# Two layers of two hybrid blocks on one core: gated attention's queries and keys turned once per token tile, the bias table stored first, the modulation without a register loop

## The chip, the cores and the metric

The kernel runs on one core of a Trainium2 chip. The metric is the device time of one execution in microseconds; lower is better. The five engines are named as in the profile: PE (TensorE, the matmuls), DVE (VectorE), ACT (ScalarE), POOL (GpSimd) and SP, which here only issues DMAs.

## What is computed

A sequence of 512 tokens of width 2048 goes through two blocks of two layers each, all in float32. The first block's layer is a projection, three kinds of attention (dense, latent, and a neighbourhood attention with a table of relative position biases `rpb`), and an output projection:

```
proj = jnp.einsum('bsd,de->bse', h, w_in)
...
s = jnp.einsum('bqhd,bqnhd->bhqn', qblk, kg).astype(jnp.float32) * scale
s = s + bblk[None].astype(jnp.float32)
...
return x + _rms_norm(y, g_post)
```

The second block's layer is modulated by a vector `c`, and one of its three branches is gated linear attention, with decays summed within chunks of 64 tokens:

```
mod = jax.nn.silu(c) @ w_mod + b_mod
...
b = jnp.cumsum(lac, axis=2)
diff = b[:, :, :, None, :] - b[:, :, None, :, :]
decay = jnp.exp(jnp.where(causal[:, :, None], diff, -jnp.inf))
scores = jnp.einsum('bhtd,bhsd,bhtsd->bhts', qc, kc, decay)
```

`w_mod` is 2048 x 6144 for each of the two layers of the second block, and does not depend on the activations.

## The kernel before

Every engine has its own instruction stream, written out by hand, and the streams meet through counting semaphores (`count(name, ...)`, `wait_ge`, `then_inc`). The main work is the projections. A panel of 512 output columns runs over 16 slices `k` of 128 input rows. For each slice, PE does 12 matmuls of 128x512: four token tiles, and three products each (`L823` to `L825`, and `L818` to `L820` where the result is wanted turned), because every float32 operand is split in a high and a low part. SP loads the weights in pairs of slices into `stage` (ring of 4), ACT takes the high part (`L1307`), DVE the low part (`L1791`), both into rings of 3.

Between the slices stands side work: after the matmuls of slice `k` of panel `p`, PE calls `side1(l, s)` (first block) or `side(l, s)` (second block). A step `s` is one slice; in the first block `s = 16 p + k`, in the second 48 less. ACT and DVE call functions of the same names at the same steps. Tables at the head of the file say which step carries what: `UNIT_AT` and `JOB_AT` the attention of the first block, `SUM_AT` the sums of the modulation, `LEVEL` the levels of gated attention.

Gated attention (second block, `LEVELS = 6` and a diagonal one, so 7 levels, for two pairs `pr` of token tiles, so 28 groups `g` per layer). For each pair and level, PE sums the logarithms of the decays with a 0/1 matrix (`decay_sums`, `L1140`), ACT exponentiates them into `eg` (`take_decays`, `L1680`), DVE multiplies queries and keys `qk_g` by them into `qke` (`decayed`, `L2561`). Then, tile by tile, PE turns the four 128x128 pieces of `qke` with the identity (`level_turns`, `L1208`), ACT copies them from PSUM to `qkT` (`L1724`), PE multiplies them to scores (`level_scores`, `L1221`), DVE masks the scores (`level_mask`, `L2576`), and POOL adds them up (`L2845`). The level steps are 74 to 78, 81 to 94 and 97 to 110. `level_turns(g)` stands in the step of index `g`, `level_scores(g - 1)` in the same one.

POOL also carries the modulation while the first block runs. `mod_panel(l, p, ring)` multiplies 16 slices of 128x512 of `w_mod` (`mod_load`, `L2751`) with the gate vector (`L2764`) and adds them up (`L2769` for the first of a panel, `L2771` for the others). There are 12 panels for each layer. PE sums a finished panel over the partitions (`mod_row_sum`, `L1009`), at the steps of `SUM_AT` for panels 0 to 8; it waits for POOL's last addition, and POOL waits to begin panel `p` until panel `p - 2` is summed, as `macc` has two buffers. POOL starts each layer of this when `CKV_READY` is reached.

The bias table of the neighbourhood attention is padded in `rpb_pad`, a strip at the end of the big buffer `zone`, then stored to `rpb_dram` (`L2791`), and read back in an expanded form by `bias_tiles` (`L2781`, eight DMAs on POOL's queue). ACT's `scores_high` (`L1545`) writes over the same end of `zone` and so waits for the store:

```
if first == 4:
    act.wait_ge(job_ev.sem, job_ev.at(0, l, J_VB + 4))
    act.wait_ge(prep.sem, prep.at(0, l, QPE_READY + 1))
    act.wait_ge(boot_rpb, 32)
```

DVE's low parts (`L2180`) come behind `scores_high`, and PE's first attention scores (`L966`, unit `U_B`, step 51) behind those.

Of the kernel before, what the change touches and what calls it, by code (L numbers as in the profile page):

```python
# [15 lines left out]
P = 128  # L16
# [101 lines left out]
QCT_AT, STATE_AT = 62, 65  # L118
PAST_AT = {67 + 2 * t: t for t in range(TT)}
# [12 lines left out]
SCALED_AT = {(64 if k == 0 else LEVEL[2 * slot_of(k) - 2]): k for k in range(2 * LEVELS)}  # L132
# [84 lines left out]
def build(nc, io, only_first=False):  # L217


    with ExitStack() as ctx:  # L220
# [182 lines left out]
        gt_done = count("gt_done", 0, 28)  # L403
        gte_done = count("gte_done", 0, 28)
# [195 lines left out]
        qcT, qkT = view(ZQ, TT, 2, P), view(ZQ, 2, 4, P)  # L600
# [9 lines left out]
        LEVELB, TURNB, OUTP = bank[4:6], bank[6], bank[7]  # L610
# [186 lines left out]
        def _(pe):  # L797
# [328 lines left out]
            def decay_sums(l, n, level, pr):  # L1126
# [12 lines left out]
                for i in range(2):  # L1139
                    mm = pe.matmul(decay_bank(n)[:, i * 256:(i + 1) * 256], gsum[:, level, :], la[:, 2 * pr + i, :],  # L1140
                                   start=True, stop=True)
# [37 lines left out]
            def past(l, t):  # L1179

                pe.wait_ge(job_ev.sem, job_ev.at(1, l, J_STATE + 2 * t + 1))
                if t == 0:
                    pe.wait_ge(ajob_ev.sem, ajob_ev.at(1, l, 7))
                else:
                    pe.wait_ge(past_ev.sem, past_ev.at(1, l, t))
# [10 lines left out]
            def level_turns(l, g, level, t):  # L1196

                s = g // 2
                if g == 0:
                    pe.wait_ge(past_ev.sem, past_ev.at(1, l, TT))  # L1200
                else:
                    pe.wait_ge(gte_done.sem, gte_done.at(1, l, g))
                if level < LEVELS:
                    pe.wait_ge(ge_done.sem, ge_done.at(1, l, 2 + (s // (LEVELS + 1)) * LEVELS + level + 1))
                for w in range(2):
                    for hp in range(2):
                        src = qk_g[:, t, w, tok(hp)] if level == LEVELS else qke[s % 2][:, t % 2, w, tok(hp)]
                        mm = pe.transpose(TURNB[:, tok(2 * w + hp)], src, ident[:, :])  # L1208
                mm.then_inc(gt_done.sem, 1)

            def level_scores(l, g):

                pe.wait_ge(gte_done.sem, gte_done.at(1, l, g + 1))
# [23 lines left out]
            def side(l, s):  # L1237
# [35 lines left out]
                if 0 <= g < 4 * (LEVELS + 1):  # L1273
                    level_turns(l, g, g // 2 % (LEVELS + 1), 2 * (g // (2 * LEVELS + 2)) + g % 2)
# [25 lines left out]
        def _(act):  # L1300
# [390 lines left out]
            def side(l, s):  # L1691
# [27 lines left out]
                g = LEVEL.index(s) if s in LEVEL else -1  # L1719
                if 0 <= g < 4 * (LEVELS + 1):  # L1720
                    act.wait_ge(gt_done.sem, gt_done.at(1, l, g + 1))
                    if g >= 2:
                        act.wait_ge(gs_done.sem, gs_done.at(1, l, g - 1))
                    act.activation(qkT[:, g % 2, :, :].rearrange("p w n -> p (w n)"), TURNB[:, :], ACT.Copy)\  # L1724
# [58 lines left out]
        def _(dve):  # L1783
# [770 lines left out]
            def decayed(l, k):  # L2554
# [3 lines left out]
                if s >= 2:  # L2558
                    dve.wait_ge(gt_done.sem, gt_done.at(1, l, 2 * (s - 1)))
# [174 lines left out]
        def _(pool):  # L2734
# [9 lines left out]
                           io["c_rpb"].rearrange("l h r c -> (l h r) c")).then_inc(boot_rpb, 16)  # L2744
            pool.wait_ge(boot_dve, 2)
# [38 lines left out]
            for l in range(2):  # L2784
# [85 lines left out]
```

## Time and profile before

| | |
|---|---|
| time, median of 3 runs | 3527.45 us (3526.79 to 3528.84) |
| the profiled execution | 3530.76 us |
| its span on the core | 3528.6 us |
| PE busy | 3432.4 us, 97% |
| DVE, ACT, POOL busy | 54%, 37%, 33% |
| mean granted clock of PE | 0.990 |

The span runs from the first to the last instruction; the 2.2 us between it and the execution's own time lie around it. PE's busy time counts overlapping matmuls once, so it says that PE always has something under way, not that it works at its peak. In the rows below a timeline row has the start, the time taken, the engine, the line and the operation, and in brackets the idle time of the engine before it and what ended it. A float32 matmul shows as two records, a transpose or a matmul of the rounded parts as one.

### The profile page before, as it was taken

How to read it: one execution, taken by the hardware profiler on the slowest of the kernel's cores; microseconds unless marked ns; L12 is line 12 of the kernel's file. 1: busy time of each engine (PE TensorE's matmuls, PEld its weight loads, DVE VectorE, ACT ScalarE, POOL GpSimd, SP SyncE). 2: the span in 40 equal slices, each digit the busy share in tenths (PEclk: the TensorE clock that was granted, in tenths of full speed). 3: DMA queues.
4: the chain of work that ended last, by engine and by line, in shares of the span. 5: the costliest groups of instructions: out<-in, count | busy, mean ns of one | idle time of the engine just before them, and what ended most of it. 6: DMA issues, size and time to landing. Idle time of an engine off the chain costs nothing.

```text
span 3528.6 us, 48194 instructions
## 1 busy us (share of the span) xinstructions
PE 3432.4 (97%) x17244; PEld 2815.9 (80%) x17244; DVE 1903.1 (54%) x3226; ACT 1317.9 (37%) x2173; POOL 1176.6 (33%) x1310
## 2 busy tenths in 40 slices
PE   8959999999999999899999999999999999999998
PEld 7638888888886788788888878878888878878887
DVE  5523486553675346665447445545547535645545
ACT  6113323332551333233337335322336435332233
POOL 0477667674205777777641000012000000002000
PEclk9979999999999999999999999999999999999999
DMA  6444454445673555444567532322446622322345
GB/s 210 144 120 120 156 154 137 133 152 177 215 231 112 144 156 148 137 136 137 197 196 220 158 66 61 98 72 60 138 157 211 189 72 61 99 71 62 120 149 185
DMA packets 225282, 490.40 MB, mean 139 GB/s; under 512 B 24254, under 2 KB 33337, under 8 KB 221224
## 3 DMA queue, kind: packets, MB, share of 16 engines
q1 hardware_dynamic: 188264, 369.13, 33.8%
q0 software_dynamic: 33632, 109.11, 10.9%
q10 hardware_dynamic: 3168, 9.24, 0.7%
q8 instruction: 138, 2.26, 0.3%
q14 instruction: 80, 0.66, 0.1%
HBM read 470.54 MB, written 20.52 MB: 139 GB/s over the span
## 4 chain that ended last, share of the span: by engine, by line
PE 89%; DVE 4%; issue 2%; POOL 2%; DMA 1%; ACT 1%; DVEq 0%; POOLq 0%; another core or an unknown queue 0%; ACTq 0%; SPq 0%
PE bank L823 23%; PE bank L825 22%; PE bank L824 22%; PE bank L986 3%; PE bank L966 3%; PE bank L975 2%; PE bank L818 1%; PE bank L820 1%; PE bank L819 1%; PE bank L949 1%; PE bank L1089 1%; DVE wlo L1791 1%; PE bank L1221 1%; PE bank L1068 1%; PE bank L846 1%
## 5 line engine op out<-in xcount | busy, mean ns | idle before, releaser
L823 PE MATMUL bank<-wlo,act_hi 128*128 128x512 f32 (+1 forms) x3712 | 1480.8, 399 | 9.5 <-DVE wlo L1791 5.7
L825 PE MATMUL bank<-whi,act_lo 128*128 128x512 f32 (+1 forms) x3712 | 1440.3, 388 | 0.0
L824 PE MATMUL bank<-whi,act_hi 128*128 128x512 f32 (+1 forms) x3712 | 1438.7, 388 | 0.0
L1791 DVE TENSOR_TENSOR wlo<-stage,whi 128x1024 fp32r<-128x1024 f32 (+1 forms) x624 | 838.0, 1345 | 776.3 <-ACT whi L1307 765.0
L1307 ACT ACTIVATE whi<-stage 128x1024 fp32r<-128x1024 f32 (+1 forms) x624 | 649.2, 1041 | 961.2 <-PE bank L825 813.8
L823 PEld LDWEIGHTS bank<-wlo,act_hi 128*128 128x128 f32 x3712 | 698.2, 188 | 171.6 <-issue 23.4
L825 PEld LDWEIGHTS bank<-whi,act_lo 128*128 128x128 f32 x3712 | 697.8, 188 | 147.6
L824 PEld LDWEIGHTS bank<-whi,act_hi 128*128 128x128 f32 x3712 | 699.3, 188 | 130.6
L2771 POOL TENSOR_TENSOR macc<-macc,mprod 128x512 f32<-128x512 f32 x360 | 504.0, 1400 | 67.5 <-POOL mprod L2764 67.5
L2751 POOL DMA_DIRECT2D wmod<-in_w_mod x384 | 222.2, 579 | 523.5 <-DVE zone L2128 298.8
L2764 POOL TENSOR_SCALAR mprod<-wmod,csil 128x512 f32<-128x512 f32 x384 | 310.3, 808 | 164.9 <-DMA wmod<-in_w_mod 82.6
L2845 POOL TENSOR_TENSOR zone<-zone 128x512 f32<-128x512 f32 x48 | 61.9, 1290 | 390.6 <-DVE zone L2576 390.6
L1531 ACT ACTIVATE zone<-bank 128x512 f32<-128x512 f32 x128 | 76.6, 598 | 233.4 <-PE bank L975 233.4
L2802 POOL CAST act_hi<-zone 128x256 fp32r<-128x256 f32 x64 | 32.8, 536 | 373.1 <-ACT zone L1462 372.4
L2827 POOL DMA_DIRECT2D macc<-in_gla_w_gate_up x4 | 2.1, 526 | 432.1 <-DVE Y L2411 432.1
L818 PE MATMUL bank<-act_hi,wlo 128*128 128x512 f32 x256 | 111.1, 434 | 0.0
L2095 DVE RECIPROCAL ri<-sm 128x1 f32<-128x1 f32 x128 | 20.5, 160 | 161.9 <-PE bank L986 160.9
L986 PEld LDWEIGHTS bank<-zone 128*128 128x128 f32 x768 | 100.3, 191 | 8.8 <-issue 1.4
L1523 ACT ACTIVATE zone<-bank,nmx,rsq 128x512 f32<-128x512 f32 x64 | 49.8, 779 | 149.1 <-DVE nmx L2087 149.1
L986 PE MATMUL bank<-zone 128*128 128x128 f32 x768 | 101.0, 274 | 1.0 <-issue 1.0
L820 PE MATMUL bank<-act_lo,whi 128*128 128x512 f32 x256 | 101.0, 394 | 0.0
L819 PE MATMUL bank<-act_hi,whi 128*128 128x512 f32 x256 | 100.8, 394 | 0.0
(280 smaller groups left out, 3274.3 us busy)
## 6 DMA issues: line engine op xcount, KB each, us to landing
stage<-in_w_in SPq DMA_DIRECT2D x400, 512.0 KB, 3.8
wmod<-in_w_mod POOLq DMA_DIRECT2D x384, 256.0 KB, 3.0
stage<-in_w_out SPq DMA_DIRECT2D x192, 512.0 KB, 4.2
out<-Y SPq DMA_DIRECT2D x48, 256.0 KB, 4.7
zone<-out SPq DMA_DIRECT2D x12, 1024.0 KB, 6.5
stage<-in_w_in SPq DMA_DIRECT2D x32, 320.0 KB, 3.1
Y<-in_x SPq DMA_DIRECT2D x4, 1024.0 KB, 9.2
zone<-in_x SPq DMA_DIRECT2D x4, 1024.0 KB, 6.6
```

Of the source, the lines that this page charges most:

```text
L818: pe.matmul(out, lo_w[:, tok(t)], hi_x, start=(k == 0), stop=False)
L819: pe.matmul(out, hi_w[:, tok(t)], hi_x, start=False, stop=False)
L820: mm = pe.matmul(out, hi_w[:, tok(t)], lo_x, start=False, stop=(k == KC - 1))
L823: pe.matmul(out, hi_x, lo_w, start=(k == 0), stop=False)
L824: pe.matmul(out, hi_x, hi_w, start=False, stop=False)
L825: mm = pe.matmul(out, lo_x, hi_w, start=False, stop=(k == KC - 1))
L986: mm = pe.matmul(bank[7][:, 0:HD], probsT[:, u % 2, tok(kt)], values(br, h, kt), start=(kt == 0), stop=(kt == TT - 1))
L1307: act.activation(whi[:, c % RH, :, 0:width], stage[:, c % RS, :, 0:width], ACT.Copy)\
L1791: dve.tensor_tensor(wlo[:, c % RH, :, 0:width], stage[:, c % RS, :, 0:width], whi[:, c % RH, :, 0:width].bitcast(F32), ALU.subtract).then_ ...
L2751: pool.dma_start(wmod[:, k % 2, :], src.rearrange("o p n -> (o p) n")).then_inc(mod_landed[k % 2].sem, 16)
L2764: pool.tensor_scalar(mprod[:, :], wmod[:, k % 2, :], csil[:, k:k + 1], 0.0, ALU.mult, ALU.add)\
L2771: pool.tensor_tensor(macc[:, ring, :], macc[:, ring, :], mprod[:, :], ALU.add).then_inc(mod_added.sem, 1)
```

## The change

There are three edits.

1. Gated attention. Queries and keys are turned once for each of the four token tiles (`turn_qk`, at the steps of `QK_TURN_AT`), and ACT writes them back over `qk_g`, now with the features on the partitions. The decays of the levels are summed with the operands exchanged, so that they too come out feature-major: four matmuls of 128 columns instead of two of 256. DVE multiplies as before, and the scores read `qke` (or `qk_g` for the diagonal level) directly. `level_turns`, `qkT` and ACT's 28 copies per layer are gone. `decayed` now waits for the scores of two slots ago instead of the turns, and the first `decayed` moves from step 64 to 66.
2. The bias table is stored right behind its load, at the head of POOL's stream, not behind the first two panels of the modulation.
3. The panels 2 to 11 of the modulation are written out for each layer instead of standing in a register loop of five rounds, and each panel's first weight load is issued within the last slice of the panel before it.

```diff
+QK_TURN_AT = {64: 0, 65: 1, 66: 2, 75: 3}
-SCALED_AT = {(64 if k == 0 else LEVEL[2 * slot_of(k) - 2]): k for k in range(2 * LEVELS)}
+SCALED_AT = {(66 if k == 0 else LEVEL[2 * slot_of(k) - 2]): k for k in range(2 * LEVELS)}
...
+        def turn_bank(t):
+            return bank[7 - t % 2]
...
                 for i in range(2):
-                    mm = pe.matmul(decay_bank(n)[:, i * 256:(i + 1) * 256], gsum[:, level, :], la[:, 2 * pr + i, :],
-                                   start=True, stop=True)
+                    if n < 4:
+                        mm = pe.matmul(decay_bank(n)[:, i * 256:(i + 1) * 256], gsum[:, level, :], la[:, 2 * pr + i, :],
+                                       start=True, stop=True)
+                        continue
+                    for hp in range(2):
+                        mm = pe.matmul(decay_bank(n)[:, tok(2 * i + hp)], la[:, 2 * pr + i, tok(hp)], gsum[:, level, :],
+                                       start=True, stop=True)
...
-            def level_turns(l, g, level, t):
-
-                s = g // 2
-                if g == 0:
+            def turn_qk(l, t):
+
+                if t == 0:
+                    pe.wait_ge(prep.sem, prep.at(1, l, QC_READY + 2))
+                if t < 2:
+                    pe.wait_ge(ajob_ev.sem, ajob_ev.at(1, l, 6 + t))
+                if t == 2:
+                    pe.wait_ge(gte_done.sem, gte_done.at(1, l, 1))
+                if t == 3:
                     pe.wait_ge(past_ev.sem, past_ev.at(1, l, TT))
-                else:
-                    pe.wait_ge(gte_done.sem, gte_done.at(1, l, g))
+                apart(pe)
+                for w in range(2):
+                    for hp in range(2):
+                        mm = pe.transpose(turn_bank(t)[:, tok(2 * w + hp)], qk_g[:, t, w, tok(hp)], ident[:, :])
+                mm.then_inc(gt_done.sem, 1)
+
+            def level_scores(l, g):
+
+                s, level, t = g // 2, g // 2 % (LEVELS + 1), 2 * (g // (2 * LEVELS + 2)) + g % 2
                 if level < LEVELS:
                     pe.wait_ge(ge_done.sem, ge_done.at(1, l, 2 + (s // (LEVELS + 1)) * LEVELS + level + 1))
...
-                        mm = pe.matmul(LEVELB[e][:, tok(hp)], qkT[half, g % 2, 2 + hp, :], qkT[half, g % 2, hp, :],
+                        mm = pe.matmul(LEVELB[e][:, tok(hp)], src[half, 1, tok(hp)], src[half, 0, tok(hp)],
...
                 if s >= 2:
-                    dve.wait_ge(gt_done.sem, gt_done.at(1, l, 2 * (s - 1)))
+                    dve.wait_ge(gs_done.sem, gs_done.at(1, l, 2 * (s - 1)))
+                if k % LEVELS == 0:
+                    dve.wait_ge(gte_done.sem, gte_done.at(1, l, 2 * pr + 2))
...
+            pool.wait_ge(boot_rpb, 16)
+            pool.dma_start(rpb_dram, rpb_pad[0:2 * C_H * RPB_R, :]).then_inc(boot_rpb, 16)
             pool.wait_ge(boot_dve, 2)
...
-                mod_load(l, p, 0)
+                if p == 0:
+                    mod_load(l, 0, 0)
                 for k in range(KC):
                     m = p * KC + k
-                    if k + 1 < KC:
-                        mod_load(l, p, k + 1)
+                    if m + 1 < NIN * KC:
+                        mod_load(l, (m + 1) // KC, (m + 1) % KC)
...
                 if l == 0:
-                    pool.wait_ge(boot_rpb, 16)
-                    pool.dma_start(rpb_dram, rpb_pad[0:2 * C_H * RPB_R, :]).then_inc(boot_rpb, 16)
                     pool.wait_ge(boot_rpb, 32)
                 bias_tiles(l)
-                with pool.Fori(1, NIN // 2) as pair:
-                    for ring in range(2):
-                        mod_panel(l, 2 * pair + ring, ring)
+                for p in range(2, NIN):
+                    mod_panel(l, p, p % 2)
```

On PE, in gated attention of the second block, this stood at the side of the level step 76 before (`L1140` sums decays, `L1208` turns, `L1221` scores):

```order
L825 MATMUL bank<-whi,act_lo 128x512
L1140 MATMUL bank<-zone 128x256 [waits ajob_ev]
L1140 MATMUL bank<-zone 128x256
L1208 MATMUL bank<-ident,zone 128x128 [waits ge_done,gte_done]
L1208 MATMUL bank<-ident,zone 128x128 x3
L1221 MATMUL bank<-zone 128x128 [waits gm_done,gte_done]
L1221 MATMUL bank<-zone 128x128 x3
L823 MATMUL bank<-wlo,act_hi 128x512
```

and at the same place of the changed kernel (where `L1149` sums decays and `L1237` scores):

```order
L829 MATMUL bank<-whi,act_lo 128x512
L1149 MATMUL bank<-zone 128x128 [waits ajob_ev]
L1149 MATMUL bank<-zone 128x128 x3
L1237 MATMUL bank<-zone 128x128 [waits gm_done,ge_done]
L1237 MATMUL bank<-zone 128x128 x3
L827 MATMUL bank<-wlo,act_hi 128x512
```

The four transposes are gone, the sums have twice as many instructions of half the columns, and the scores wait for DVE's product instead of ACT's copy.

On DVE, around the same step, the order stays, and one wait is another. Before (`L1791` low parts of weights, `L2561` product with the decays, `L2576` mask):

```order
L1791 TENSOR_TENSOR wlo<-stage,whi 128x1024 [waits w_used,hi_done]
L2561 TENSOR_TENSOR zone<-zone 128x512 [waits gt_done,ajob_ev]
L2561 TENSOR_TENSOR zone<-zone 128x512
L2576 TENSOR_TENSOR zone<-bank,zone 128x256 [waits gs_done]
L2576 TENSOR_TENSOR zone<-bank,zone 128x256
```

and now:

```order
L1808 TENSOR_TENSOR wlo<-stage,whi 128x1024 [waits w_used,hi_done]
L2580 TENSOR_TENSOR zone<-zone 128x512 [waits gs_done,ajob_ev]
L2580 TENSOR_TENSOR zone<-zone 128x512
L2595 TENSOR_TENSOR zone<-bank,zone 128x256 [waits gs_done]
L2595 TENSOR_TENSOR zone<-bank,zone 128x256
```

The two products now stand behind the scores of the same step, and the masks of those scores behind the products.

On POOL, behind the second panel of the first layer, this stood before:

```order
L2791 DMA rpb_pad<-zone 120x127 [waits boot_rpb,mod_added]
L2781 DMA rpb_tiles<-rpb_pad 14x64x64 [waits boot_rpb]
L2781 DMA rpb_tiles<-rpb_pad 14x64x64 x7
L2794 UNCONDITIONAL_BRANCH
L2794 ISA
L2751 ISA [waits mod_used]
L2751 DMA wmod<-in_w_mod 128x512
L2749 REGISTER_ALU
L2751 ISA [waits mod_used]
L2751 DMA wmod<-in_w_mod 128x512
L2760 ISA
L2762 REGISTER_ALU [waits mod_landed0]
```

and now:

```order
L2772 DMA wmod<-in_w_mod 128x512 [waits mod_used,mod_added]
L2786 TENSOR_SCALAR mprod<-wmod,csil 128x512 [waits mod_landed1]
L2793 TENSOR_TENSOR macc<-macc,mprod 128x512 [waits mod_used]
L2803 DMA rpb_tiles<-rpb_pad 14x64x64 [waits boot_rpb,mod_added]
L2803 DMA rpb_tiles<-rpb_pad 14x64x64 x7
L2772 DMA wmod<-in_w_mod 128x512 [waits mod_used]
L2786 TENSOR_SCALAR mprod<-wmod,csil 128x512 [waits mod_landed0,mod_sum]
L2791 COPY macc<-mprod 128x512 [waits mod_used]
```

The store of the table is gone from here, the next panel's first load stands ahead of the bias tiles, and no register instruction stands between the slices.

## Rows read from the trace of the kernel before

**Rows 1.** The page: busy time of the engines and their shares of the span.

```profile
PE 3432.4 (97%) x17244; PEld 2815.9 (80%) x17244; DVE 1903.1 (54%) x3226; ACT 1317.9 (37%) x2173; POOL 1176.6 (33%) x1310
```

**Rows 2.** Waits of PE, longest first: us in total, times, longest.

```profile
PE bank L966 <- DVE zone_r L2180: 43.3, 1, 43.3
PE bank L1009 <- issue: 9.9, 1, 9.9
```

**Rows 3.** Timeline of POOL and ACT at the end of the 43 us wait.

```profile
234.77 0.59 POOL L2791 DMA_DIRECT2D rpb_pad<-zone  x1 [0.29 <-POOL macc L2771]
...
236.81 1.15 ACT L1545 ACTIVATE zone_r<-zone 128x512 fp32r<-128x512 f32 x2 [48.89 <-DMA rpb_pad<-zone]
```

**Rows 4.** Timeline: two points of PE's program, in the first layer, then the second.

```profile
155.14 3.67 PE L949 MATMUL bank<-zone 128*128 128x512 f32 x8 [0.67 <-issue]
...
248.47 0.95 PE L1009 MATMUL bank<-ones,macc 128*128 128x1 f32 x8
...
1107.89 3.67 PE L949 MATMUL bank<-zone 128*128 128x512 f32 x8 [0.71 <-issue]
...
1155.43 0.95 PE L1009 MATMUL bank<-ones,macc 128*128 128x1 f32 x8
```

**Rows 5.** Timeline, second layer: DVE's last low parts and PE's first scores.

```profile
1148.05 2.87 DVE L2180 TENSOR_TENSOR zone_r<-zone,zone_r 128x512 fp32r<-128x512 f32 x2
...
1151.06 0.94 PE L966 MATMUL bank<-zone_r,Y_r 128*128 128x512 f32 x3
```

**Rows 6.** Timeline: PE's sums of panels 5 and 6, first layer, then second.

```profile
535.41 0.95 PE L1009 MATMUL bank<-ones,macc 128*128 128x1 f32 x8
624.29 0.95 PE L1009 MATMUL bank<-ones,macc 128*128 128x1 f32 x8
...
1451.71 1.84 PE L1009 MATMUL bank<-ones,macc 128*128 128x1 f32 x8 [9.88 <-issue]
1543.49 0.94 PE L1009 MATMUL bank<-ones,macc 128*128 128x1 f32 x8
```

**Rows 7.** Stretch behind the 43 us wait; behind POOL's busy time stands PE's granted clock.

```profile
241.00:247.00 6.00, 5.48 (x12) 3.65 (x13) 2.39 (x4) 1.72 (x3) 3.65 (x6) 0.50 0.99 267
```

**Rows 8.** Timeline of POOL, second layer: first additions of panels 0, 1, 2, 6.

```profile
1088.01 0.61 POOL L2769 COPY macc<-mprod 128x512 f32<-128x512 f32 x1 [0.17 <-POOL mprod L2764]
...
1142.38 0.61 POOL L2769 COPY macc<-mprod 128x512 f32<-128x512 f32 x1 [0.17 <-POOL mprod L2764]
...
1211.00 0.61 POOL L2769 COPY macc<-mprod 128x512 f32<-128x512 f32 x1 [0.18 <-POOL mprod L2764]
...
1456.86 0.61 POOL L2769 COPY macc<-mprod 128x512 f32<-128x512 f32 x1 [0.17 <-POOL mprod L2764]
```

**Rows 9.** Timeline of POOL: a pause at a load in the loop.

```profile
688.18 0.54 POOL L2751 DMA_DIRECT2D wmod<-in_w_mod  x1 [2.80 <-issue]
```

**Rows 10.** Timeline of PE: side work of the level steps 76 and 77.

```profile
2337.66 1.02 PE L1140 MATMUL bank<-zone 128*128 128x256 f32 x4
2338.52 0.60 PE L1208 MATMUL bank<-ident,zone 128*128 128x128 f32 x4
2339.05 0.72 PE L1221 MATMUL bank<-zone 64*128 64x128 f32 x8
...
2343.11 0.71 PE L1221 MATMUL bank<-zone 64*128 64x128 f32 x8
```

**Rows 11.** Timeline of PE: four float32 matmuls of 128 columns (chunk output).

```profile
2472.04 1.05 PE L1233 MATMUL bank<-zone 128*128 128x128 f32 x8
2472.85 0.48 PE L823 MATMUL bank<-wlo,act_hi 128*128 128x512 f32 x1
```

**Rows 12.** Timeline of DVE and POOL in the level steps 76 and 77.

```profile
2337.01 1.29 DVE L2561 TENSOR_TENSOR zone<-zone 128x512 f32<-128x512 f32 x2
2339.82 0.76 DVE L2576 TENSOR_TENSOR zone<-bank,zone 128x256 f32<-128x256 f32 x2 [1.52 <-PE bank L1221]
...
2344.71 1.28 POOL L2845 TENSOR_TENSOR zone<-zone 128x512 f32<-128x512 f32 x1 [105.17 <-DVE zone L2576]
```

More of the change, by code:

```diff
@@ L402, in build @@
         ge_done = count("ge_done", 0, 2 + 2 * LEVELS)
-        gt_done = count("gt_done", 0, 28)
-        gte_done = count("gte_done", 0, 28)
+        gt_done = count("gt_done", 0, TT)
+        gte_done = count("gte_done", 0, TT)
         gs_done = count("gs_done", 0, 28)
@@ L599, in build @@
         kt_g, qc_g = view(PP + 3072, TT, 256), view(ZQ + 2048, TT, 256)
-        qcT, qkT = view(ZQ, TT, 2, P), view(ZQ, 2, 4, P)
+        qcT = view(ZQ, TT, 2, P)
         eg = view(ZQ + 1024, 2, 2, 256)
@@ L609, in build @@
         turn_tmp = view(ZV, TT, SEQ)
-        LEVELB, TURNB, OUTP = bank[4:6], bank[6], bank[7]
+        LEVELB, OUTP = bank[4:6], bank[7]
+        def turn_bank(t):
+            return bank[7 - t % 2]
         def decay_bank(n):
@@ L1183, in past @@
                     pe.wait_ge(ajob_ev.sem, ajob_ev.at(1, l, 7))
+                    pe.wait_ge(gte_done.sem, gte_done.at(1, l, 3))
                 else:
@@ L1194, in past @@
                 mm.then_inc(past_done.sem, 1)
-            def level_turns(l, g, level, t):
-                s = g // 2
-                if g == 0:
-                    pe.wait_ge(past_ev.sem, past_ev.at(1, l, TT))
-                else:
-                    pe.wait_ge(gte_done.sem, gte_done.at(1, l, g))
+            def turn_qk(l, t):
[6 more added lines that the diff above has]
+                if t == 3:
+                    pe.wait_ge(past_ev.sem, past_ev.at(1, l, TT))
+                apart(pe)
[5 more added lines that the diff above has]
+                s, level, t = g // 2, g // 2 % (LEVELS + 1), 2 * (g // (2 * LEVELS + 2)) + g % 2
                 if level < LEVELS:
                     pe.wait_ge(ge_done.sem, ge_done.at(1, l, 2 + (s // (LEVELS + 1)) * LEVELS + level + 1))
[L1205 to L1213, printed above, removed]
+                else:
+                    pe.wait_ge(gte_done.sem, gte_done.at(1, l, t + 1))
+                src = qk_g[:, t, :, :] if level == LEVELS else qke[s % 2][:, t % 2, :, :]
                 if g == 0:
@@ L1272, in side @@
                 g = LEVEL.index(s) if s in LEVEL else -1
-                if 0 <= g < 4 * (LEVELS + 1):
-                    level_turns(l, g, g // 2 % (LEVELS + 1), 2 * (g // (2 * LEVELS + 2)) + g % 2)
+                if s in QK_TURN_AT:
+                    turn_qk(l, QK_TURN_AT[s])
                 if 1 <= g <= 4 * (LEVELS + 1):
@@ L1718, in side @@
                     take_decays(l, 5 + k, k % 2)
[L1719 to L1724, printed above, removed]
+                if s in QK_TURN_AT:
+                    t = QK_TURN_AT[s]
+                    if t == 0:
+                        act.wait_ge(prep.sem, prep.at(1, l, QC_READY + 2))
+                        act.wait_ge(ge_done.sem, ge_done.at(1, l, 2))
+                    act.wait_ge(gt_done.sem, gt_done.at(1, l, t + 1))
+                    act.activation(qk_g[:, t, :, :].rearrange("p w n -> p (w n)"), turn_bank(t)[:, :], ACT.Copy)\
                        .then_inc(gte_done.sem, 1)
```

## The prediction

> **What bounds the kernel now.** I read the page first: PE is busy for 97% of the span, the other engines for 54% or less [rows 1]. So only two things can shorten this kernel: less work on PE, or less waiting of PE. Next the list of PE's waits [rows 2]. Two of its entries concern the change: one wait of 43.3 us of the first attention scores (`L966`) on DVE's low parts `L2180`, and one of 9.9 us in `mod_row_sum` (`L1009`), which the profile puts down to "issue". The timeline of the engines behind the first [rows 3] leads past DVE: ACT's high part `L1545` sat idle for 48.9 us until the DMA of the padded table landed, and POOL had issued that DMA at 234.77, straight behind an addition of the modulation. The DMA itself took about 2 us; what was late was its place in POOL's program, behind two panels. The "issue" of the second wait is an unnamed releaser; the function waits for POOL's additions, and POOL began its next panel at 1456.86, 5 us behind PE's start at 1451.71 [rows 6, 8], so its last addition fits the release.
>
> **The bias table.** The second layer runs the same program without the store. From the matmuls `L949` to the first sum `L1009` the layers differ so: the distance between the layers is 1107.89 - 155.14 = 952.75 at the first point and 1155.43 - 248.47 = 906.96 at the second [rows 4]. The first layer loses 45.8 us in between: the wait, and about 2.5 us behind it, in which PE ran at a granted clock of 0.50, its 1.2 GHz level [rows 7]. With the table stored at the start nothing of that is left, and the first layer should run as the second does. What is late next is seen there: DVE ended its last pair of low parts at 1150.92 and PE began the scores at 1151.06 [rows 5], so DVE is the next releaser, with next to nothing to wait for; that fraction is inside the 45.8. The store's own cost at the head of POOL's stream is nothing: POOL then waits anyway until the first panel may begin, and the load is covered by PE's first matmuls.
>
> **The modulation.** PE's wait in the second layer is sized in the same way. The distance between the layers grows from 906.96 to 1451.71 - 535.41 = 916.30 at the sum of panel 5 and to 1543.49 - 624.29 = 919.20 at that of panel 6 [rows 4, 6]: 12.2 us. It matters that edit 2 puts the first layer 45.8 us forward on PE and leaves POOL's start where it is: then the first layer, which had no such wait, stands as the second does, and would get one too. So edit 3 has to remove 12.2 us and to prevent another 12.2.
>
> Does it? PE wanted the sum of panel 5 at 1451.71 - 9.88 = 1441.8. In the loop POOL took (1456.86 - 1211.00) / 4 = 61.5 us per panel; panels 0 and 1 are straight code already, and from one to the next it took 1142.38 - 1088.01 = 54.4 [rows 8], with the wait for the panel's first load that now is issued a slice earlier. Four panels of 54.4 from 1211.0 end at 1428.6: PE finds the sum ready with 13 us to spare, and more with the earlier load. I take both waits as gone. The limit is 59.0 us per panel (61.5 - 9.9 / 4). The bias tiles go out as before, in the second layer without a wait of PE.
>
> In the loop POOL also paused, once for 2.80 us, for nothing that the profile names [rows 9]. The Trainium skill, Runtime: NRT & Kernel Launch, section Instruction fetch mechanics, says that fetch is sequential and that a taken branch outside the buffered pages stalls for a fetch, which favours written-out code; by that rule the straight pace holds for all panels and the sum stays as it is.
>
> **Gated attention.** Each group of four transposes moved PE's next work by 2339.05 - 2338.52 = 0.53 us [rows 10]. 28 go and 4 come for each layer: 24 x 0.53 = 12.7, in two layers 25.4 us. PE has no cover for them: none of its listed waits of any size is in this part. The sums with exchanged operands: two float32 matmuls of 256 columns took 2338.52 - 2337.66 = 0.86 [rows 10]; four of 128 columns with a stationary operand each took 2472.85 - 2472.04 = 0.81 [rows 11]. By busy time they are 1.02 and 1.05. For 24 sums that is between -1.2 and +0.7 us; I take 0. ACT's 24 fewer copies per layer were beside PE's work and bring nothing.
>
> What the edit adds is DVE's wait: the products `decayed` now wait for the scores of the same step, and the masks stand behind them, which PE's next scores need. Before, from the start of the scores to the end of the masks it took 2339.82 + 0.76 - 2339.05 = 1.53 us [rows 10, 12]. The two products add 1.29: 2.82. PE's next scores came 2343.11 - 2339.05 = 4.06 behind, and without the transposes come 3.53 behind. So 0.7 us is left, and PE does not wait. Where a level step is the last but one of a panel (four places) the gate's work on DVE slides too, for at most 0.5 us each; that is 0 to 2 us, taken as 0.
>
> **Sum.** 45.8 + 12.2 + 25.4 = 83.4. From the profiled execution's 3530.76 that gives 3447.4. Its time is 3.3 us above the median of the runs, 3527.45; for the median I predict **3444.0 us**, 2.4% less.
>
> **Rivals.**
>
> *POOL stays at the loop's pace* (59 us or more per panel), because its pace comes from DMA landings or from DVE and not from the loop. Against it stands 54.4 measured beside the same DVE work; for it, that this is one panel, with fewer other transfers than later ones. Then both layers wait 12.2: the second as before, the first newly. 3444.0 + 24.4 = 3468.4; with one layer only 3456.
>
> *DVE becomes the bound in the level steps.* Ten of the products per layer wait for scores. If POOL's addition, 1.28 us [rows 12], holds them up each time, the chain is 2.82 + 1.28 = 4.10 against 3.53: 0.6 x 20 = 12 us, 3456. Against it: POOL's addition begins when the masks end, and its 1.28 us are over before the next scores, 3.53 behind. The Trainium skill, SBUF — State Buffer, section Who interferes with whom, says that a DVE instruction with two SBUF inputs contends for a shared port with a GpSimd instruction that reads SBUF, and one blocks fully; that rule is what would make this case. The rows show such a cost in the first block: the pair of `L2180` took 2.87 us with POOL at work [rows 5], against 1.29 for two products of this size [rows 12]. Two more such pairs held up ahead of the first scores would cost 3.2 us per layer, up to 6 in all, 3450.
>
> *The store is not what held PE:* another wait takes its place, as of the weights or of DVE. Then the 45.8 stay, and the time is 3490. Against it: the second layer has the same program and no wait.
>
> *Slower than before.* POOL's written-out code of ten panels per layer could be fetched too slowly. If it took x us per panel, the sum of panel 5 would come 4 (x - 59.0) late in each layer. From x = 69.5 on this is 41.7 per layer and eats the whole gain; at 75 it is 64 per layer, and the time 3572. Nothing speaks for it but the length of the code; the two straight panels show 54.4.
>
> **Chances.** The forecast 0.74, with its own range of 3439 to 3450 from the bounds above (-1.2 to +0.7 for the sums, up to 2 for the gates, some of the 6 for the port); POOL's pace 0.11; DVE's chain or port 0.09; the store not the cause 0.03; slower 0.02; the remaining 0.01 is a gain of another size below. The range of 3438 to 3462 holds the forecast, DVE's chain and POOL's wait in one layer. A measurement of this kernel tells about 0.2% (7 us) from no change. All cases but the slower one gain more than that; with a little for a mishap between: faster 0.96, same 0.02, slower 0.02.
>
> **What would show it.** `L966` without the 43 us wait, and the distance between the layers at the first `L1009` near 952.7. No wait at any `L1009`, and POOL's panels 2 to 11 from 50 to 55 us apart. Records of the turns down from 224 to 32, the level steps 0.53 us closer, no wait of PE at the scores on `level_mask` or `decayed`, and PE's granted clock at 1.00 through the first block. The prediction is wrong if POOL's panels are over 59 us apart, if the masks end more than 3.5 us behind the start of the scores, or if another wait stands ahead of `L966`.

## The result

The changed kernel took 3464.68 us (median of 4 runs, 3463.31 to 3470.07), the kernel before 3528.14 in the runs beside it (3526.79 to 3533.76). The ratio is 0.982 with an interval of 0.9803 to 0.9837. It is faster by 63.5 us, 1.8%; 83.4 were forecast, 2.4%, and the time lies 2.7 us above the range. The profiled execution took 3470.07 us, 60.7 less than that of before, and the gap of 22.7 us to the forecast is looked for in it. It is the slowest of the four; two later series of the same kernel are 70.6 and 69.0 us faster than the kernel before.

The page of the changed kernel, to be put beside [rows 1]:

```profile
PE 3412.8 (98%) x17148; PEld 2798.4 (81%) x17148; DVE 1901.6 (55%) x3226; ACT 1294.5 (37%) x2125; POOL 1198.2 (35%) x1310
```

PE's busy time fell by 19.6 us and the rest of the gain is idle time. The list of PE's waits, which answers to [rows 2], now begins with

```profile
PE bank L970 <- DVE q_hl L2084: 11.5, 2, 6.0
```

and goes on with the entries that it had below those of [rows 2], of 9.0 us and less. The wait of 43.3 us is gone, and so is the one at the modulation's sums (`L1013`, before `L1009`). The one at the top is new: attention scores, now `L970`, waited twice for DVE's low part of a query head, `q_hl`. The timeline of PE shows both, with the sums of panels 0, 4, 5 and 11 of the first layer and 0, 5 and 11 of the second:

```profile
201.75 0.95 PE L1013 MATMUL bank<-ones,macc 128*128 128x1 f32 x8
...
441.39 0.94 PE L1013 MATMUL bank<-ones,macc 128*128 128x1 f32 x8
490.28 1.65 PE L970 MATMUL bank<-k_hl,q_hl 128*128 128x512 f32 x3 [5.50 <-DVE q_hl L2084]
496.33 0.95 PE L1013 MATMUL bank<-ones,macc 128*128 128x1 f32 x8
...
908.75 0.94 PE L1013 MATMUL bank<-ones,macc 128*128 128x1 f32 x8
...
1118.88 0.95 PE L1013 MATMUL bank<-ones,macc 128*128 128x1 f32 x8
...
1407.93 1.65 PE L970 MATMUL bank<-k_hl,q_hl 128*128 128x512 f32 x3 [6.01 <-DVE q_hl L2084]
1414.22 0.95 PE L1013 MATMUL bank<-ones,macc 128*128 128x1 f32 x8
...
1826.48 0.95 PE L1013 MATMUL bank<-ones,macc 128*128 128x1 f32 x8
```

Reading a gain along a program is subtracting the same instruction's start in both traces. The matching rows of the kernel before are in [rows 4, 6] and these:

```profile
488.05 0.94 PE L1009 MATMUL bank<-ones,macc 128*128 128x1 f32 x8
531.84 0.98 PE L966 MATMUL bank<-k_hl,q_hl 128*128 128x512 f32 x3 [0.39 <-DVE q_hl L2067]
...
945.70 0.95 PE L1009 MATMUL bank<-ones,macc 128*128 128x1 f32 x8
...
1438.27 0.84 PE L966 MATMUL bank<-k_hl,q_hl 128*128 128x512 f32 x3
...
1865.55 0.95 PE L1009 MATMUL bank<-ones,macc 128*128 128x1 f32 x8
```

The lead over the kernel before is 46.7 us at the first sum (248.47 - 201.75) and at that of panel 4. At panel 5 it is 39.1, at panel 11 of the first layer 37.0. In the second layer it is 36.6 at the first sum, 37.5 at panel 5 and 39.1 at the last, where removing the old wait should have added 12.2. So behind the first sum the changed kernel lost 9.7 us in the first layer and gained 2.5 in the second. Before, the second layer's PE waited 9.88 us at the sum [rows 6] and not for `q_hl`; now it waits 6.01 for `q_hl` and not at the sum.

The wait costs more than its length. From the sum of panel 4 to that of panel 5 it now takes 496.33 - 441.39 = 54.94 us, where it took 535.41 - 488.05 = 47.36: 7.6 more, for 5.1 more of waiting. The stretch behind the wait (columns as in [rows 7]):

```profile
490.20:493.00 2.80, 2.72 (x6) 2.15 (x7) 0.88 (x3) 0.11 (x1) 2.27 (x4) 0.50 0.75 216
```

PE came out of its idle time at a granted clock of 0.50, the 1.2 GHz level.

### The profile page after: what moved, and what is told of

The parts are those of the page before. It is cut to its first block, busy times and chain, and to the rows that moved or that the text cites. A ratio compares the mean times of both kernels' runs of the same rounds, so it can differ in the third digit from the quotient of the medians.

```text
span 3468.3 us, 46705 instructions
## 1 busy us (share of the span) xinstructions
PE 3412.8 (98%) x17148; PEld 2798.4 (81%) x17148; DVE 1901.6 (55%) x3226; ACT 1294.5 (37%) x2125; POOL 1198.2 (35%) x1310
## 4 chain that ended last, share of the span: by engine, by line
PE 92%; DVE 5%; issue 2%; ACT 1%; DMA 0%; DVEq 0%; POOL 0%; ACTq 0%; SPq 0%
PE bank L827 23%; PE bank L829 22%; PE bank L828 22%; PE bank L990 3%; PE bank L970 3%; PE bank L953 2%; PE bank L822 2%; PE bank L824 2%; PE bank L823 2%; PE bank L979 2%; DVE wlo L1808 1%; PE bank L1093 1%; PE bank L1237 1%; PE bank L1072 1%; PE bank L850 1%
## 5 line engine op out<-in xcount | busy, mean ns | idle before, releaser
L1808 DVE TENSOR_TENSOR wlo<-stage,whi 128x1024 fp32r<-128x1024 f32 (+1 forms) x624 | 815.8, 1310 | 778.7 <-ACT whi L1323 767.8
L2864 POOL TENSOR_TENSOR zone<-zone 128x512 f32<-128x512 f32 x48 | 83.7, 1743 | 348.3 <-DVE zone L2595 348.3
L990 PEld LDWEIGHTS bank<-zone 128*128 128x128 f32 x768 | 100.0, 191 | 12.1 <-issue 5.0
```

The costliest lines, as they stand in the source:

```text
L990: mm = pe.matmul(bank[7][:, 0:HD], probsT[:, u % 2, tok(kt)], values(br, h, kt), start=(kt == 0), stop=(kt == TT - 1))
L1808: dve.tensor_tensor(wlo[:, c % RH, :, 0:width], stage[:, c % RS, :, 0:width], whi[:, c % RH, :, 0:width].bitcast(F32), ALU.subtract).then_ ...
```

## The experiments

The eleven runs below fall in three groups; the kernels of a group ran on one chip beside the same runs of the kernel before. Group one is the first four, group two the next four. Two of the eleven are the changed kernel again, and one is the kernel with panel 6 held again.

### The three edits apart

**Edit 2 alone.** The kernel before with the store at the head:

```diff
+            pool.wait_ge(boot_rpb, 16)
+            pool.dma_start(rpb_dram, rpb_pad[0:2 * C_H * RPB_R, :]).then_inc(boot_rpb, 16)
             pool.wait_ge(boot_dve, 2)
...
                 if l == 0:
-                    pool.wait_ge(boot_rpb, 16)
-                    pool.dma_start(rpb_dram, rpb_pad[0:2 * C_H * RPB_R, :]).then_inc(boot_rpb, 16)
                     pool.wait_ge(boot_rpb, 32)
```

> The kernel before with the table stored first and nothing else. Alignment theory (the first layer moves 45.8 us forward on PE and then runs as the second did): the 43 us wait is gone, and the first layer gets the second layer's wait of 9.9 us at the sum of panel 5, worth 12.2 us. Time 3528.1 - 45.8 + 12.2 = 3494.5, gain 33.6. Rival (the first layer needs no new wait): 3482. Rival (another wait takes the store's place): 3528.

Measured: 3493.19 us against 3530.39, ratio 0.9891 (0.9874 to 0.9907). Its two waits at the sum of panel 5, by the timeline of PE:

```profile
495.05 1.84 PE L1009 MATMUL bank<-ones,macc 128*128 128x1 f32 x8 [6.42 <-issue]
...
1417.40 1.84 PE L1009 MATMUL bank<-ones,macc 128*128 128x1 f32 x8 [9.85 <-issue]
```

The first layer, put forward on PE, got a wait that it had not had: the step of the prediction holds. It is 6.4 us long and not 9.9. From the sum of panel 4 to that of panel 6 the first layer now takes 587.74 - 441.81 = 145.93 us, and took 624.29 - 488.05 = 136.24 without the wait: 9.7 us to prevent, not 12.2. The time came close to the 3494.5 expected although this term was 2.5 too large.

**Edit 3 alone.** The kernel before with the panels written out and each panel's first load issued within the panel before:

```diff
-                mod_load(l, p, 0)
+                if p == 0:
+                    mod_load(l, 0, 0)
...
-                with pool.Fori(1, NIN // 2) as pair:
-                    for ring in range(2):
-                        mod_panel(l, 2 * pair + ring, ring)
+                for p in range(2, NIN):
+                    mod_panel(l, p, p % 2)
```

> The kernel before with the ten panels written out and each panel's first load a slice earlier; table and gated attention as before. Port theory (POOL's denser work slows DVE's two-input operations, and DVE's first query parts come late): the second layer gains only 2 to 3 of its 12.2 us, because PE waits 5 to 6 us for q_hl there instead of 9.9 for POOL, and the first layer loses 5 to 9 us where it had 0.4 us of wait for q_hl; together about 3528 to 3533, no gain. Rival (the late q_hl has nothing to do with POOL's pace): the second layer gains 12.2, the first keeps its 0.4 us, 3516.

Measured: 3524.74 us, ratio 0.9987 (0.9977 to 0.9997). Its waits of PE hold the old 43.3 us and a small new one:

```profile
PE bank L966 <- DVE q_hl L2067: 2.5, 2, 2.2
```

The result lies between the two expectations. The wait at the sum went, but the medians show a gain of only 5.7 us of 12.2. The profiled execution is the fastest of the ten (3519.34 to 3530.07), so its wait of 2.2 us may be shorter than that of the others.

**Edit 1 alone.** The changed kernel with the store and the loop as before.

> The kernel before with the new gated attention alone. As predicted at 0.53 us per group of transposes: 25.4 us less, 3502.7. By the changed kernel's trace, where PE's scores behind the main matmuls start 0.09 us later than the turns did and behind the sums 0.12 us later, a group is worth 0.44 or 0.41 us: 10.1 us per layer, 3508.0.

Measured: 3511.95 us (3506.85 to 3517.52), ratio 0.994 (0.9919 to 0.9961), 18.4 us less than before, against the prediction's 25.4. Two of the four runs took 3507 us and two 3517, and the profiled one is the slowest. In it PE waited 5.9 us at the sum of panel 2 and 6.5 at that of panel 5 in the second layer, and its last sum comes at 1867.72, 2.2 us later than before. So 18.4 is not the worth of the level steps alone: they took 186.6 us in each layer of this trace, 10.0 less than before (the stretch is given below).

**Edits 1 and 2.** The changed kernel with the loop, and each panel's load, as before.

> The changed kernel with the register loop back (edits 1 and 2). Alignment theory: PE waits about 9.9 us for the sum of panel 5 in both layers and not for q_hl; 3528.1 - 33.6 - 20.1 = 3474.4, so the written-out panels are worth 10 us in the changed kernel, not the 24.4 of the prediction. Rival (the late q_hl comes with the shifted first layer, not with POOL's pace): PE waits for q_hl with the loop too.

Measured: 3473.75 us (3471.63 to 3476.58), ratio 0.9837 (0.982 to 0.9854). Its list of waits has the sums and not `q_hl`:

```profile
PE bank L1013 <- issue: 13.0, 2, 6.5
```

It differs from the changed kernel by edit 3 alone, and by 9 us, not 24.4 (these two medians are of different groups). In the two profiled executions the last sum comes at 1826.75 and 1826.48 us: up to there edit 3 brought 0.3 us in this pair. It removes this wait and puts another in its place.

### What holds up `q_hl`

DVE makes `q_hl` behind a run of work that takes nearly all its time. The kernel with edits 1 and 2 is the right one to compare with, since it has POOL's loop and stands at the same place of the program at the same time. One view groups DVE's instructions ahead of `q_hl` (columns: line, engine, operation, out<-in, count | busy us, mean ns | idle us before them). The kernel with edits 1 and 2, from 434 to 487 us:

```profile
L1808 DVE TENSOR_TENSOR wlo<-stage,whi 128x1024 fp32r<-128x1024 f32 x9 | 13.3, 1474 | 3.2 <-ACT whi L1323 3.2
...
L2145 DVE TENSOR_TENSOR Y<-zone 128x512 f32<-128x512 f32 x4 | 5.7, 1414 | 0.1
```

The changed kernel, from 434 to 490:

```profile
L1808 DVE TENSOR_TENSOR wlo<-stage,whi 128x1024 fp32r<-128x1024 f32 x9 | 16.3, 1816 | 1.4 <-ACT whi L1323 1.4
L2145 DVE TENSOR_TENSOR Y<-zone 128x512 f32<-128x512 f32 x4 | 6.4, 1603 | 0.1
...
L2251 DVE TENSOR_REDUCE ss<-zone 128x4 f32<-128x512 f32 x4 | 2.5, 670 | 0.0
```

The same instructions take longer. POOL is denser there, as the windows show (PE, PEld, DVE, ACT and POOL busy, PE's clock, DMA share, GB/s), with edits 1 and 2 and then in the changed kernel:

```profile
434.00:487.00 53.00, 53.00 (x245) 43.94 (x244) 47.45 (x69) 13.51 (x19) 38.57 (x43) 1.00 0.55 163
```

```profile
434.00:487.00 53.00, 50.78 (x234) 41.77 (x232) 51.56 (x62) 13.57 (x18) 44.92 (x47) 1.00 0.51 160
```

POOL went from 38.57 to 44.92 us busy of 53, DVE from 47.45 to 51.56, and it got through fewer instructions. Two theories: POOL's arithmetic holds DVE up, or the weight loads that it issues do. Three kernels tell them apart, with the changed kernel run again beside them.

> The changed kernel once more, beside the next three. The waits for q_hl were 5.5 and 6.0 us in its first profile and 2.2 in the run with the written-out panels alone; if they depend on how the operations of POOL and DVE happen to fall, they differ here again, between 1 and 8 us each, and the time is 3463 to 3470.

Measured: 3463.83 us (3457.89 to 3466.3) against 3534.44, ratio 0.98 (0.9783 to 0.9816); the two waits for `q_hl` came to 8.6 us.

**Short additions.** Three panels' additions cut to 16 columns. The other 496 columns of the sums of these panels are left out:

```diff
-                        pool.tensor_tensor(macc[:, ring, :], macc[:, ring, :], mprod[:, :], ALU.add).then_inc(mod_added.sem, 1)
+                        n = 16 if p in (4, 5, 6) else PW
+                        pool.tensor_tensor(macc[:, ring, 0:n], macc[:, ring, 0:n], mprod[:, 0:n], ALU.add).then_inc(mod_added.sem, 1)
```

> The changed kernel with POOL's additions of the modulation panels 4, 5 and 6 cut from 512 to 16 columns (the rest of those sums is left out); loads and multiplications are whole. Port theory: DVE's two-input operations ahead of q_hl are held up less, PE does not wait for q_hl in either layer, and the time falls by the waits and PE's slow clock behind them, 10 to 18 us, to 3447 to 3455. Rival (the weights of the modulation on the DMA queues slow DVE's inputs): the loads come no later than before, the waits stay, 3465.

Measured: 3452.58 us (3451.15 to 3454.13), ratio 0.9774 (0.9757 to 0.979), with no wait for `q_hl`. The same groups of DVE, from 434 to 483 us:

```profile
L1808 DVE TENSOR_TENSOR wlo<-stage,whi 128x1024 fp32r<-128x1024 f32 x9 | 11.0, 1226 | 9.5 <-ACT whi L1323 9.4
...
L2145 DVE TENSOR_TENSOR Y<-zone 128x512 f32<-128x512 f32 x4 | 2.8, 692 | 0.1
...
L2251 DVE TENSOR_REDUCE ss<-zone 128x4 f32<-128x512 f32 x4 | 2.5, 674 | 0.0
```

1816 and 1603 ns fell to 1226 and 692, the reduction stayed, and DVE now has 9.4 us of idle time in which it waits for ACT. POOL's multiplications ran on (17 in this window, 944 ns each), so most of it is the additions, which read two inputs. The multiplications hold DVE up too, for less. In this kernel, the first of these two ran beside no multiplication and the second beside one that began at 444.02 and took 0.70 us:

```profile
442.59 0.42 DVE L2145 TENSOR_TENSOR zone<-zone 128x256 f32<-128x256 f32 x1
443.91 1.09 DVE L2145 TENSOR_TENSOR zone<-zone 128x256 f32<-128x256 f32 x1
```

An estimate of the whole counts, for each of DVE's instructions of the stretch ahead of `q_hl` (the windows of the groups above), what it took beyond the shortest one of its line and shape in the run (leaving out less than 0.06 us): 21.9 us in the changed kernel, 13.6 with edits 1 and 2, 4.8 here.

**Short loads.** The same three panels with loads of 16 columns; the rest of `wmod` keeps what it held:

```diff
-                pool.dma_start(wmod[:, k % 2, :], src.rearrange("o p n -> (o p) n")).then_inc(mod_landed[k % 2].sem, 16)
+                n = 16 if p in (4, 5, 6) else PW
+                pool.dma_start(wmod[:, k % 2, 0:n], src.rearrange("o p n -> (o p) n")[:, 0:n]).then_inc(mod_landed[k % 2].sem, 16)
```

> The changed kernel with the loads of the modulation panels 4, 5 and 6 cut from 512 to 16 columns (the rest of each slice is stale), POOL's multiplications and additions whole. Port theory: POOL is as dense as before or denser, the waits for q_hl stay, 3463 to 3470. Rival (DMA traffic): the waits go, 3450.

Measured: 3464.95 us (3460.99 to 3466.53), ratio 0.9805 (0.9789 to 0.9822). PE waited 7.9 us for `q_hl` in two waits. The window of the changed kernel, then its own:

```profile
434.00:482.00 48.00, 48.00 (x223) 39.86 (x222) 46.91 (x51) 13.57 (x18) 40.66 (x42) 1.00 0.50 155
```

```profile
434.00:482.00 48.00, 48.00 (x223) 39.84 (x222) 47.34 (x56) 13.03 (x17) 40.78 (x42) 1.00 0.31 83
```

The moved bytes fell from 155 to 83 GB/s, and DVE and POOL stayed as busy. With short additions they rose to 184 GB/s (434 to 483 us), and DVE was quicker. The rival of the transfers falls.

**Panel 6 held.** POOL begins panel 6 only when the first query head is done; nothing is left out:

```diff
                     if k == 0:
                         pool.wait_ge(mod_sum.sem, mod_sum.at(0, l, p - 1))
+                        if p == 6:
+                            pool.wait_ge(job_ev.sem, job_ev.at(0, l, J_AQ + 1))
```

> The changed kernel with POOL's panel 6 held back until DVE's first query parts are done (job_ev of the first query head). POOL then leaves DVE alone for the last 15 to 20 us of the stretch ahead of q_hl, and panel 6 is still ready 15 us or more ahead of its sum. Port theory: the wait for q_hl falls to 0 to 3 us in each layer; 4 to 10 us faster than the changed kernel, 3455 to 3461. Rival: the waits stay, 3465.

Measured: 3456.58 us (3453.18 to 3460.62), ratio 0.9787 (0.9771 to 0.9804), with no wait for `q_hl`. The last 17 us ahead of it, from 465 to 482, in the changed kernel and then in this one:

```profile
465.00:482.00 17.00, 17.00 (x79) 14.10 (x78) 16.86 (x19) 3.19 (x3) 14.40 (x15) 1.00 0.54 170
```

```profile
465.00:482.00 17.00, 17.00 (x79) 14.05 (x77) 14.56 (x32) 3.18 (x3) 4.38 (x5) 1.00 0.53 156
```

POOL is out of the way for most of it, and DVE has time to spare. The four runs overlap those of the changed kernel beside them (3457.89 to 3466.30), so the kernel is run once more below. This is a remedy, not only a probe: nobody needs panel 6 so early.

### The level steps, and the remedy again

**Wide sums.** The changed kernel, with the decays of the levels summed as before, two matmuls of 256 columns with the tokens on the partitions. The numbers summed are then not those that the levels want; the work has the size of before:

```diff
-                    if n < 4:
+                    if n < 17:
                         mm = pe.matmul(decay_bank(n)[:, i * 256:(i + 1) * 256], gsum[:, level, :], la[:, 2 * pr + i, :],
```

> The changed kernel with the decays of the levels summed as before, two matmuls of 256 columns each, token-major (the products then mix up features and tokens, so the scores of gated attention are other numbers). The trace of the changed kernel has 0.98 us from the start of four 128-column sums to the scores behind them, against 0.86 for the old form ahead of the turns. If the exchanged operands cost that 0.12 us, 24 sums give back up to 2.9 us and the step is 0.86 again; if the cost lies in the scores' own start behind float32 sums of any form, the step stays near 0.98 and the time at that of the changed kernel. Either way PE's scores behind the rounded matmuls stay 0.77 us behind.

Measured: 3458.57 us (3453.61 to 3461.43) against 3530.24, ratio 0.9795 (0.9778 to 0.9811). The changed kernel and the held one ran beside it in five rounds each:

> The changed kernel beside the held one: 3462 to 3466, with waits for q_hl of 2 to 6 us in each layer.

Measured: 3461.28 us (3455.09 to 3466.99), ratio 0.9806 (0.979 to 0.9822), waits for `q_hl` 7.2 us.

> The held panel 6 again, in more rounds beside the changed kernel, for an interval: 3453 to 3460, 5 to 9 us below the changed kernel, without a wait for q_hl in the profile.

Measured: 3451.67 us (3449.36 to 3454.84), ratio 0.9783 (0.977 to 0.9797), no wait for `q_hl`. This is the fastest complete kernel here: 9.6 us less than the changed one beside it (7.2 in the group before), 2.2% less than the kernel before. In this group the runs of the two kernels do not overlap. POOL's price for it, by the timeline of the held kernel:

```profile
482.55 0.69 POOL L2788 TENSOR_SCALAR mprod<-wmod,csil 128x512 f32<-128x512 f32 x1 [6.73 <-DVE q_hl L2084]
...
1390.46 0.69 POOL L2788 TENSOR_SCALAR mprod<-wmod,csil 128x512 f32<-128x512 f32 x1 [12.86 <-DVE q_hl L2084]
```

POOL idled for 6.7 and 12.9 us, and no sum of a later panel was late for it.

For the level steps, the timeline of PE in the changed kernel, one group alone and one behind the sums:

```profile
2302.70 0.39 PE L829 MATMUL bank<-whi,act_lo 128*128 128x512 f32 x1
2303.02 0.72 PE L1237 MATMUL bank<-zone 64*128 64x128 f32 x8
2303.66 0.50 PE L827 MATMUL bank<-wlo,act_hi 128*128 128x512 f32 x1
...
2306.52 1.05 PE L1149 MATMUL bank<-zone 128*128 128x128 f32 x8
2307.50 0.72 PE L1237 MATMUL bank<-zone 64*128 64x128 f32 x8
2308.15 0.50 PE L827 MATMUL bank<-wlo,act_hi 128*128 128x512 f32 x1
```

and of the kernel before, at the same two kinds of place:

```profile
2342.34 0.40 PE L825 MATMUL bank<-whi,act_lo 128*128 128x512 f32 x1
2342.57 0.60 PE L1208 MATMUL bank<-ident,zone 128*128 128x128 f32 x4
...
2343.75 0.50 PE L823 MATMUL bank<-wlo,act_hi 128*128 128x512 f32 x1
...
2360.96 1.02 PE L1140 MATMUL bank<-zone 128*128 128x256 f32 x4
2361.82 0.60 PE L1208 MATMUL bank<-ident,zone 128*128 128x128 f32 x4
...
2362.99 0.50 PE L823 MATMUL bank<-wlo,act_hi 128*128 128x512 f32 x1
```

From the last main matmul to the next one it took 2343.75 - 2342.34 = 1.41 us and takes 2303.66 - 2302.70 = 0.96: 0.45 less. From the sums it took 2.03 and takes 1.63: 0.40 less. Neither is 0.53: scores behind main matmuls start 0.32 after them, where transposes started 0.23 after. Not every float32 matmul does so: the chunk outputs (`L1249`), float32 too, start 0.23 behind a main matmul. Why the scores differ stays open. Nor is most of it the exchanged sums: in the kernel with wide sums the scores start 0.95 us behind them,

```profile
2290.13 1.02 PE L1145 MATMUL bank<-zone 128*128 128x256 f32 x4
2291.08 0.71 PE L1237 MATMUL bank<-zone 64*128 64x128 f32 x8
```

against 0.98 with the new sums and 0.86 from wide sums to transposes before. So of the 0.12 us lost behind sums, 0.03 is the exchange and 0.09 the scores' own start. Over the whole stretch of the level steps the wide sums save 0.24 us per layer (186.29 against 186.53). The median of this kernel is 2.7 us below that of the changed one beside it, but the runs overlap, and 0.5 of that at most comes from the level steps.

## Why the prediction was right and wrong

**The bias table: right.** 45.8 us forecast, 46.7 of lead at the first sum, 0.5 of it there from the start. With edit 2 alone, and its new wait in the first layer, the time came out 1.3 us from what the steps gave.

One of its signs was worked out wrongly: the distance between the layers at the first sum was to be near 952.7 us. The old wait lies ahead of that sum in the first layer, so its removal puts both layers forward alike, and the distance stays at 906.96. It is 1118.88 - 201.75 = 917.13, longer by what the first layer now loses behind the sum. The forecast did not use it.

**POOL's pace: right.** Forecast was 54.4 us per panel and a limit of 59.0. The first additions of panels 2 and 6, by the timeline of POOL:

```profile
1165.70 0.61 POOL L2791 COPY macc<-mprod 128x512 f32<-128x512 f32 x1 [0.17 <-POOL mprod L2786]
...
1385.18 1.48 POOL L2791 COPY macc<-mprod 128x512 f32<-128x512 f32 x1 [0.17 <-POOL mprod L2786]
```

(1385.18 - 1165.70) / 4 = 54.9. No sum waited. The rival of POOL's pace is out although the time came near its 3468: the number alone would have given it the case, the list of waits does not.

**"I take both waits as gone": the step that failed.** The two waits at the sums went, but the prediction put the cost of POOL's denser work for DVE ahead of `q_hl` at nothing, and a new wait came there, 5.5 us in the first layer and 6.0 in the second. The term of this step in the sum is +12.2 us between the first sum and the end of the first block; measured, the lead fell from 46.7 to 39.1 there, -7.6. In the two later profiles of the same kernel the new waits came to 8.6 and 7.2 us, and the term to -1.0 and -1.2. With panel 6 held it was +9.0 and, in the second series, +12.1. Less was there to prevent, too (9.7 us and not 12.2 in the first layer with edit 2 alone). The prediction knew the cause: its rival of DVE's port names it, and priced it in the level steps and at `L2180`. It did not look at the stretch where POOL would be newly dense. That stretch could be read before: PE's scores there already waited 0.39 us for `q_hl` in the first layer; in the second DVE ended `q_hl` at 1437.73, 0.5 us ahead of the scores at 1438.27. A POOL that makes a panel in 55 us and not in 61.5 works more in every microsecond, and DVE pays. The Trainium skill, SBUF — State Buffer, section Who interferes with whom, says that a DVE instruction with two SBUF inputs contends with a GpSimd instruction that reads SBUF, and that a reduction does not; the trace agrees for the additions (1816 ns against 1226) and the reduction (670 against 674).

Between the sums of panels 4 and 5 this costs 7.6 us in the first layer. In the second the stretch took 1414.22 - 1358.52 = 55.70 us, 8.3 more than the 47.36 of the first layer before, 15.9 together. From the sum of panel 5 to that of panel 6 another 0.9 and 0.8 go (89.75 and 89.68 us, for 88.88 in the first layer before). From panel 6 to 7 it is 2.0 in the first layer (68.46 for 66.49), with two idle times of 1.1 us each in it, and 0.6 in the second (68.35 for 67.72); neither was tried apart. The remedy's result fits: without the wait the gain is 3534.44 - 3456.58 = 77.9 and 3530.24 - 3451.67 = 78.6 us, the forecast less the next term's error 78.1.

The sign "PE's granted clock at 1.00 through the first block" failed with it (0.50 behind the new wait).

**Gated attention: right in kind, off in size.** No wait of PE stands at the scores, and DVE was not the bound: where the products come first, the masks end 2.80 us behind the start of the scores (forecast: 2.82), and PE's next scores come 3.59 behind at the soonest (2303.02 - 2299.43; forecast: 3.53):

```profile
2308.34 1.29 DVE L2580 TENSOR_TENSOR zone<-zone 128x512 f32<-128x512 f32 x2 [2.67 <-ACT zone L1696]
2309.55 0.75 DVE L2595 TENSOR_TENSOR zone<-bank,zone 128x256 f32<-128x256 f32 x2
```

Here the scores started at 2307.50, and the masks ended at 2310.30. The profile names ACT's exponentials as what released this product and most others, and PE's scores for two in each layer; the masks end as far behind the scores in both cases. So the gates and the port cost nothing there. The term "24 x 0.53" took the distance from transposes to scores for what a group of transposes costs. What PE does next starts later without them, and a group was worth 0.40 to 0.45. The stretch from the chunk sums to the last chunk output took 2478.39 - 2281.80 = 196.59 us and takes 186.53, by the start of its first and last rows: 10.1 us per layer, 20.1 in both, where 25.4 were forecast. The exchanged sums cost 0.03 us where scores follow, 0.24 per layer by the kernel with wide sums, inside the bounds given. There are 29 level steps, the last of them 106 and not 110.

**The account, by the lead over the kernel before.** The table and the start give 46.7 us. By the end of the first block 12.2 were to be added, 58.9; the lead is 39.1. Of the 19.8 missing, the two waits for `q_hl` with the slow clock behind them are 15.9, the stretches from panel 5 to 6 1.7, those from 6 to 7 2.6, and small gains elsewhere take 0.4 off. The level steps add 20.1 of 25.4. The difference of the spans is 60.3 (3528.6 - 3468.3), so 1.1 is left for the rest of the second block; a wait of 0.6 us that went (`L1068`) is part of it. This is the account of the slowest run of four: with waits of 7.2 us instead of 11.5, in the last profile, the lead at the last sum was 45.7.

## What to carry to other kernels

When an edit makes one engine work more densely, find the stretches where its neighbour is nearly always busy (DVE for 47.45 of 53 us with the loop) and someone waits for it at their end, before counting the gain: ahead of `q_hl` DVE had nothing to spare in the first layer and 0.5 us in the second, and that was to be read from two rows. If its instructions there read two inputs from SBUF, as POOL's do, hold the work that is not urgent until that stretch is over; one wait on POOL was worth 7 to 10 us here. And a removed instruction is worth the time between the main matmuls around it with and without it, not the distance to its neighbour.

## What was not expected of the hardware

In the stretch ahead of `q_hl` the nine low parts of 128x1024 took either 1.22 to 1.24 us or 2.18 to 2.32. Two of them in the changed kernel, by the timeline of DVE, and an addition, by that of POOL:

```profile
447.97 2.32 DVE L1808 TENSOR_TENSOR wlo<-stage,whi 128x1024 fp32r<-128x1024 f32 x1
456.69 1.24 DVE L1808 TENSOR_TENSOR wlo<-stage,whi 128x1024 fp32r<-128x1024 f32 x1
```

```profile
447.63 1.58 POOL L2793 TENSOR_TENSOR macc<-macc,mprod 128x512 f32<-128x512 f32 x1 [0.19 <-POOL mprod L2786]
```

The addition ran on for 1.24 us beside the first of them, which took 1.1 us longer than the second. This fits an instruction that stands still while the other engine reads. Over the whole program low parts of all lengths between 1.2 and 2.3 us occur (109 of 592 are over 1.25), so two lengths are no rule.

With the additions cut to 16 columns all nine took 1.22 to 1.24, though POOL's multiplications, with one SBUF tensor as input, went on beside them. There POOL waited as well: its multiplication at 447.04 took 2.27 us, where an undisturbed one takes 0.70, beside a low part that began at 447.00 and took 1.23. But smaller DVE products of the same kernel were held up by multiplications (1.09 us for 0.42, above). What decides which of the two engines waits was not tried by itself.

The length of the new wait differs between executions of one kernel: 5.5 and 6.0 us in the first profile, 0.95 and 6.21 in the last. That fits two engines whose relative place decides which instruction meets which (argued, not tried), and the changed kernel's runs (3455.1 to 3467.0 in five rounds) scatter more than those of the held one (3449.4 to 3454.8).
